# A hybrid attention and RWKV-7 step on one core: one small store ahead of a load, one activation ahead of a copy, and the stores at a stage's end on SyncE

## The chip, the cores and the metric

The kernel runs on one core of a Trainium2 chip. The core has five engines with an instruction queue each: TensorE (PE, with its weight loads shown as PEld), VectorE (DVE), ScalarE (ACT), GpSimd (POOL) and SyncE (SP), which here issues most DMAs. The engines wait for each other through semaphores. The metric is the device time of one execution in microseconds; the median of the runs of a kernel counts.

## The reference, cut to what matters

One layer of a streaming encoder is computed for a prompt of 2048 rows and for 8 running streams of 16 rows each (together 17 tiles of 128 rows, tile 16 being the streams):

```python
proj = rms_norm(h, norm_gain) @ w_in
att, rcols, g_r = split_projection(proj)
q, k, v, g_a = attn_qkv(att, q_norm_gain, k_norm_gain)
o_a = chunk_band_attention(q, k, v, rel_pos_bias)       # streams: attention over a cache
prev = jnp.concatenate([jnp.zeros_like(rcols[:, :1]), rcols[:, :-1]], axis=1)
o_r, S = rwkv_branch(rcols, prev, S0, g_r, ...)          # a recurrence over time with state S
z = jnp.concatenate([o_a * silu(g_a), o_r], axis=-1)     # o_r holds silu(g_r) already
h = h + z @ w_out
```

The outputs are both updated sequences, the new keys and values, the recurrent states and the last projected rows.

## The kernel before, in words

`program` runs four stages, one after the other. Each is a block of instruction streams, one for each engine. At a block's end all engines meet, GpSimd clears the block's semaphores (`clear_semaphores`), and only then does the next block's first instruction run on any engine. Waits for stores whose semaphores are in `Shared` are left to the end of the last block.

1. `attention_phase` (about 0 to 545 us): for each tile the q, k, v projection (each fp32 product as three products of fp32r halves, "hi" and "lo"), the norms and the chunked attention. Beside it the normalised, transposed x is made for the later stages: ScalarE finds each row's 1/rms (`norm_stats`), SyncE stores those 128 numbers in memory (`store_rstd`, L233) and reads them back spread over all partitions (`load_row`, L238), GpSimd multiplies (`norm_x`, L337 and L340), and SyncE stores the tile (`store_xT`, L246). `load_x` (L225) brings the next tile's rows for ScalarE; it waits for the sum of squares of the tile before, and `store_rstd` for that tile's finished 1/rms, two small ScalarE instructions later.
2. `rwkv_projection_phase` (to about 855 us): the token-shifted projection.
3. `rwkv_phase` (to about 1567 us): the recurrence, with the gate projection beside it. Its instruction order is written as generators: each `yield` gives a place on a scale of some 40 units for a tile, and `merged` takes the pieces of all generators of an engine in the order of these numbers. In the last step (t = DEC = 16) `out` begins the output product for tiles 0 and 1: `split_w` halves w_out into `out_w_hi` (ScalarE) and `out_w_lo` (GpSimd for k = 0 and 1, VectorE after), `open_gates` applies silu to a tile's gates (`z_gate`), `store_y` writes y.
4. `output_phase` (about 1568 us to the end): the output product for the other 15 tiles, and the cached attention of the 8 streams.

At the end of stage 3 these meet: `store_y(0, j)` on SyncE; the new states of the streams (`out_wkv_sample_new`, L1501, two stores); the rows of `o_rwkv` of tile 16 (`tail`, L1490, four stores), which stage 4 reads back only for its last tile; and the two halves of y of tile 1, stored by ScalarE (L1776) after VectorE's last additions (`add_x(1, j)`, L1951), the second of which ends VectorE's stream.

Of the kernel before, what the change touches and what calls it, by code (L numbers as in the profile page):

```python
# [22 lines left out]
P = 128  # L23
D = 1024
# [34 lines left out]
def rows_of(dram, width):  # L59

    return dram.rearrange("b s d -> (b s) d")
# [70 lines left out]
def attention_phase(nc, io, shared):  # L132
    with ExitStack() as ctx:
# [88 lines left out]
        def _(sp):  # L222
            def load_x(n):
                wait(sp, x_sumsq, n)
                sp.dma_start(x_tok[:], x_rows(n)).then_inc(x_loaded, 16)  # L225

            def load_xT(n):
                wait(sp, xT_stored, 16 * (n - 2))
                sp.dma_start(xT[n % 3][:], io["x_T"][n]).then_inc(xT_loaded[n % 3], 16)

            def store_rstd(n):
                sp.wait_ge(x_rstd, n + 1)
                sp.dma_start(io["rstd"][n].rearrange("(p o) -> p o", o=1), rstd[:, n:n + 1]).then_inc(rstd_stored, 16)  # L233

            def load_row(n):
                sp.wait_ge(rstd_stored, 16 * (n + 1))
                wait(sp, x_by_row, n)
                sp.dma_start(row[:], io["rstd"][n].rearrange("(o p) -> o p", o=1).broadcast_to([P, P])).then_inc(row_loaded, 16)  # L238
# [5 lines left out]
            def store_xT(n):  # L244
                sp.wait_ge(x_normed, n + 1)
                sp.dma_start(io["xT"][n], xT[n % 3][:]).then_inc(xT_stored, 16)  # L246

            def store_kv(t):
                rows = slice((t - 12) * P, (t - 11) * P)
                sp.wait_ge(k_kept, t - 11)  # L250
                sp.dma_start(io["k_prompt_new"][0, 0, :, rows, :].rearrange("h s d -> s h d"),
                             k_out[:].rearrange("p (h d) -> p h d", h=H)).then_inc(k_stored, 16)
                sp.wait_ge(proj_read, 3 * (t + 1))
                sp.dma_start(io["v_prompt_new"][0, 0, :, rows, :].rearrange("h s d -> s h d"),
                             v[:, t % RING, :].rearrange("p (h d) -> p h d", h=H)).then_inc(v_stored, 16)

            def store_o(t):
                sp.wait_ge(out_ready, t + 1)
                sp.dma_start(io["o_att"][t * P:(t + 1) * P, :], o_tok[:].rearrange("p h d -> p (h d)")).then_inc(out_stored, 16)
# [34 lines left out]
            for t in range(TILES):  # L294
                more = t + 2 <= DEC
                if t >= 12:
                    store_kv(t)
                if t + 3 <= DEC:
                    load_x(t + 3)
                if more:  # L300
                    store_rstd(t + 2)
                    load_row(t + 2)
                if t > 1:
                    store_o(t - 2)
                if more:
                    store_xT(t + 2)
                if t + 5 <= DEC:
                    load_xT(t + 5)
# [785 lines left out]
def rwkv_phase(nc, io, shared):  # L1094

    with ExitStack() as ctx:
# [5 lines left out]
        def sem(name):  # L1102
            held.append(ctx.enter_context(nc.semaphore("r_" + name)))
            return held[-1]

        def sb2(name, shape):
            return [sb(f"{name}{i}", shape) for i in range(2)]

        def sems2(name):
            return [sem(f"{name}{i}") for i in range(2)]  # L1110
# [49 lines left out]
        gate_out = sb2("gate_out", [P, AW])  # L1160
# [83 lines left out]
        go_loaded, x_half_loaded, y_stored = sems2("go_loaded"), sems2("x_half_loaded"), shared.y_stored  # L1244
        z_opened, z_gated, z_turned, z_hi_ready, z_lo_ready = sem("z_opened"), sem("z_gated"), sem("z_turned"), sem("z_hi_ready"), sem("z_lo_ready")
        y_summed, y_added = sem("y_summed"), sem("y_added")
# [63 lines left out]
        OUT_X = tuple(slice(j * 512, (j + 1) * 512) for j in range(2))  # L1310
# [19 lines left out]
        LAST_TAIL = 34  # L1330
# [46 lines left out]
        def _(sp):  # L1377
# [32 lines left out]
            def load_out_w(k):  # L1410
                sp.dma_start(out_raw[k % 4][:].rearrange("p k n -> p (k n)"), io["w_out"][0, k * P:(k + 1) * P, :]).then_inc(shared.out_w_loaded[k % 4], 16)
# [7 lines left out]
            def load_x_half(n, j):  # L1419
                sp.dma_start(gate_out[j][:], rows_of(io["x_prompt"], D)[n * P:(n + 1) * P, OUT_X[j]]).then_inc(x_half_loaded[j], 16)  # L1420

            def store_y(n, j):
                sp.wait_ge(y_added, 2 * n + j + 1)
                sp.dma_start(rows_of(io["y_prompt"], D)[n * P:(n + 1) * P, OUT_X[j]], gate_out[j][:]).then_inc(y_stored[j], 16)
# [29 lines left out]
            def out(t, u, mode):  # L1454
                yield 0
                for k in range(4, KT):
                    sp.wait_ge(shared.out_w_lo, k - 3)
                    load_out_w(k)
                for j in range(2):
                    sp.wait_ge(gate_stored[j], 16 * (DEC + 1))  # L1460
                    load_x_half(0, j)
                yield 19
                for n in range(2):
                    sp.wait_ge(z_turned, 2 * n + 2)
                    load_go(2 + n, shared.g_loaded[n], shared.o_loaded[n])
                for j in range(2):
                    yield 31 + j
                    store_y(0, j)
                    sp.wait_ge(y_stored[j], 16)
                    load_x_half(1, j)  # L1470

            def mix(t, u, mode):

# [8 lines left out]
                load_xs(t, u, slice(0, 4), r_loaded)  # L1482

            def tail(t, u, mode):
                yield 17.5 if mode == "p" else 45.5 - LAST_TAIL
                need(sp, t, "out")
                for n in range(NCH):
                    rows = io["o_rwkv"][t * P + n * CH:t * P + (n + 1) * CH, :].rearrange("l (c g d) -> g l c d", g=2, d=HD)
                    for g in range(2):
                        sp.dma_start(rows[g], y_tok[half(g), cols_of(n)].rearrange("p (c d) -> p c d", c=PAIRS)).then_inc(o_stored, 16)  # L1490
# [124 lines left out]
        def _(act):  # L1615
# [116 lines left out]
            def open_gates(n, loaded, opened):  # L1732
                act.wait_ge(loaded, 48 if loaded is go_loaded[n % 2] else 16)
                nc.scalar.activation(z_gate[n % 2][:], z_gate[n % 2][:], ACT.Silu).then_inc(opened, 1)

            def out(t, u, mode):
                def split_w(k):
                    if k == 0:
                        act.wait_ge(gate_written, 2 * (DEC + 1))
                    act.wait_ge(shared.out_w_loaded[k % 4], 16 * (k // 4 + 1))  # L1740
                    nc.scalar.activation(out_hi[:, k, :], out_raw[k % 4][:].rearrange("p k n -> p (k n)"), ACT.Copy).then_inc(shared.out_w_hi, 1)

                def round_z(n, i):
                    act.wait_ge(z_turned, 2 * n + i + 1)
                    nc.scalar.activation(z_hi[n][:, 4 * i:4 * i + 4, :].rearrange("p k n -> p (k n)"), ps_job[i][:], ACT.Copy).then_inc(z_hi_ready, 1)

                yield 0.2
                split_w(0)
                open_gates(0, go_loaded[0], z_opened)
                split_w(1)  # L1750
                yield 3.3
                open_gates(1, go_loaded[1], z_opened)
                for i in range(2):
                    round_z(0, i)
                yield 7.35
                for k in range(2, 4):
                    split_w(k)
                yield 8.5
                for k in range(4, KT):
                    split_w(k)  # L1760
                yield 10.6
                for i in range(2):
                    round_z(1, i)
                yield 22
                for n in range(2):
                    open_gates(2 + n, shared.g_loaded[n], shared.silu_ready)
                act.preload_act_table_set(ACT_TABLES)
                for i in range(2):
                    yield 31.6 + 2 * i
                    act.wait_ge(y_summed, 2)  # L1770
                    act.wait_ge(z_turned, 5 + i)
                    nc.scalar.activation(x_hi[:, 4 * i:4 * i + 4, :].rearrange("p k n -> p (k n)"), ps_job[1][:], ACT.Copy).then_inc(shared.z_first_hi, 1)
                for j in range(2):
                    yield 50 + j
                    act.wait_ge(y_added, 2 + j + 1)
                    act.dma_start(rows_of(io["y_prompt"], D)[P:2 * P, OUT_X[j]], gate_out[j][:]).then_inc(y_stored[j], 16)  # L1776

            tiles(act, front, back, mix, tail, gates, first_gates, out)

# [931 lines left out]
```

## Time and profile before

| | |
|---|---|
| median of 3 runs | 1772.42 us (1771.13 to 1773.47) |
| the profiled execution | 1771.13 us, its span 1769.3 us |
| PE busy | 1707.2 us (96%), mean granted clock 0.985 |
| DVE, ACT, POOL busy | 828.6, 799.4, 417.3 us |
| bytes moved by DMA | 170.88 MB, mean 97 GB/s |

The span runs from the first to the last instruction of the profiled execution; the time of the execution is 1.8 us more. A row's "[idle before <- releaser]" says how long its engine sat idle and what ended that. SPq and ACTq are DMA issues on the queues of SyncE and ScalarE: their duration is the time of the issue, not of the transfer. A merged row ("x4") stands for several instructions in a row, from the start of the first.

### The profile page before, as it was taken

Reading aid. Unit: us, or ns where it says so; the run is one execution under the profiler, and the core shown is the slowest. Engines: PE = TensorE matmul, PEld = TensorE weight load, DVE = VectorE, ACT = ScalarE, POOL = GpSimd, SP = SyncE. Lnnn points to the kernel's source line nnn. Section 1 sums busy time; section 2 is a strip of 40 time slices with the busy share of each in tenths; the row PEclk is TensorE's granted clock in tenths of the full one; section 3 lists DMA queues with packets and bytes.
Section 4 is the critical chain, followed back from the end, with each engine's and each line's share of the span. In section 5 each row is a group of like instructions: output and inputs, shape, how many; then the busy total and the mean of one; then the engine's idle time right before and its main releaser. Section 6 shows DMA issues by size and latency. Waiting matters only on the chain. (4 is left out here: it accounts for less than half of the span.)

```text
span 1769.3 us, 48548 instructions
## 1 busy us (share of the span) xinstructions
PE 1707.2 (96%) x21338; PEld 1398.7 (79%) x21338; DVE 828.6 (47%) x1198; ACT 799.4 (45%) x1656; POOL 417.3 (24%) x282
## 2 busy tenths in 40 slices
PE   6999999999998999999889999999999999889999
PEld 5778888888887888999667777787777777667787
DVE  4345444444444311223446565555565556643432
ACT  5556666665655322223434444444444444423420
POOL 3332221122110000000213544334454334320000
PEclk9999999999999999999889999999999999899999
DMA  6322211112134412214311212212212213466652
GB/s 228 110 73 81 59 52 68 56 57 74 44 109 174 154 61 87 85 61 146 112 48 52 72 52 66 67 52 63 60 52 75 58 53 108 143 252 230 205 176 87
DMA packets 119138, 170.88 MB, mean 97 GB/s; under 512 B 39568, under 2 KB 78992, under 8 KB 118672
## 3 DMA queue, kind: packets, MB, share of 16 engines
q1 hardware_dynamic: 109280, 152.76, 26.8%
q10 hardware_dynamic: 9648, 15.01, 2.3%
q8 instruction: 169, 2.77, 0.7%
q14 instruction: 41, 0.34, 0.1%
HBM read 113.21 MB, written 55.06 MB: 95 GB/s over the span
## 5 line engine op out<-in xcount | busy, mean ns | idle before, releaser
L652 PE MATMUL a_ps_proj<-a_w_hi,a_x_hi 128*128 128x512 f32 x384 | 155.8, 406 | 0.0
L652 PE MATMUL a_ps_proj<-a_w_hi,a_x_lo 128*128 128x512 f32 x384 | 150.2, 391 | 0.0
L652 PE MATMUL a_ps_proj<-a_w_lo,a_x_hi 128*128 128x512 f32 x384 | 149.6, 390 | 0.0
L1056 DVE SCALAR_TENSOR_TENSOR j_out<-j_ps,j_rest,j_part 128x512 f32<-128x512 f32 (+2 forms) x65 | 41.9, 645 | 220.4 <-ACT j_last_cols L1004 170.0
L562 DVE SCALAR_TENSOR_TENSOR a_stage<-a_ps_s,a_new_bias 128x256 f32<-128x256 f32 x64 | 27.2, 424 | 229.0 <-PE a_ps_s L679 229.0
L2222 PE MATMUL r_ps_gate<-gate_w_hi,gate_x_hi 128*128 128x512 f32 x272 | 116.5, 428 | 4.6 <-PEq L66 3.4
L2222 PE MATMUL r_ps_gate<-gate_w_lo,gate_x_hi 128*128 128x512 f32 x272 | 116.4, 428 | 0.0
L2222 PE MATMUL r_ps_gate<-gate_w_hi,gate_x_lo 128*128 128x512 f32 x272 | 116.3, 428 | 0.0
L1002 ACT ACTIVATE j_part<-j_last_cols,j_shift_in 128x1 f32<-128x1 f32 x65 | 19.2, 296 | 212.8 <-PE j_ps L1081 212.8
L1862 DVE TENSOR_TENSOR r_w_mat<-r_ps_w,consts 128x512 f32<-128x512 f32 x83 | 57.3, 691 | 106.0 <-PE r_ps_w L2106 106.0
L337 POOL TENSOR_TENSOR a_xT<-a_xT,a_row 128x1024 f32<-128x1024 f32 x17 | 40.4, 2374 | 251.6 <-DMA a_row<-scratch_rstd 241.0
L445 ACT ACTIVATE a_stage<-a_stage,a_small 128x640 f32<-128x640 f32 (+4 forms) x128 | 95.9, 753 | 0.9 <-DVE a_small L570 0.9
L679 PEld LDWEIGHTS a_ps_s<-a_kT,a_qT 64*128 64x128 f32 x592 | 59.8, 186 | 33.1 <-issue 28.0
L570 DVE TENSOR_REDUCE a_small<-a_stage 128x2 f32<-128x1280 f32 (+4 forms) x64 | 84.5, 1320 | 2.2
L652 PEld LDWEIGHTS a_ps_proj<-a_w_hi,a_x_lo 128*128 128x128 f32 x384 | 72.1, 188 | 16.1
L652 PEld LDWEIGHTS a_ps_proj<-a_w_lo,a_x_hi 128*128 128x128 f32 x384 | 72.4, 189 | 13.3
L679 PE MATMUL a_ps_s<-a_kT,a_qT 64*128 64x128 f32 (+3 forms) x592 | 81.7, 389 | 1.0 <-ACT a_kT L436 0.8
L652 PEld LDWEIGHTS a_ps_proj<-a_w_hi,a_x_hi 128*128 128x128 f32 x384 | 72.2, 188 | 13.2 <-issue 0.2
L454 ACT ACTIVATE a_stage<-a_ps_p 128x1024 f32<-128x1024 f32 (+3 forms) x60 | 56.5, 942 | 52.9 <-PE a_ps_s L701 52.9
L713 PE MATMUL a_ps_out<-a_stage,a_v 128*64 128x128 f32 x1120 | 75.3, 278 | 1.4 <-ACT a_stage L456 1.4
L1511 POOL MEMSET r_g_run<- 128x544 f32 x1 | 0.6, 557 | 308.2 <-POOLq L66 308.2
L713 PEld LDWEIGHTS a_ps_out<-a_stage,a_v 128*64 128x64 f32 x1120 | 59.8, 136 | 9.5 <-ACT a_stage L456 1.6
(383 smaller groups left out, 4690.2 us busy)
## 6 DMA issues: line engine op xcount, KB each, us to landing
a_xT<-in_x_T SPq DMA_DIRECT2D x17, 512.0 KB, 3.6
scratch_xT<-a_xT SPq DMA_DIRECT2D x17, 512.0 KB, 2.6
raw<-scratch_xT SPq DMA_DIRECT2D x17, 512.0 KB, 4.6
scratch_gates<-r_gate_out SPq DMA_DIRECT2D x34, 256.0 KB, 2.4
z_gate<-scratch_gates SPq DMA_DIRECT2D x17, 512.0 KB, 4.3
xs<-scratch_xs_T SPq DMA_DIRECT2D x15, 576.0 KB, 4.3
a_x<-in_x_prompt SPq DMA_DIRECT2D x16, 512.0 KB, 4.5
scratch_xs_T<-j_out ACTq DMA_DIRECT2D x39, 192.0 KB, 1.9
```

The costliest lines, as they stand in the source:

```text
L337: nc.gpsimd.tensor_tensor(xT[n % 3][:], xT[n % 3][:], by_token, ALU.mult).then_inc(x_by_row, 1)
L445: nc.scalar.activation(probs[s % 2][:, e, lo * P:WIN], probs[s % 2][:, e, lo * P:WIN], ACT.Exp, bias=neg_max[s % 2][:, e:e + 1], accum_out ...
L454: nc.scalar.activation(pT[:, :, lo:SLOTS - 1, :].rearrange("p e j n -> p e (j n)"), ps_p[:].rearrange("p (e n) -> p e n", e=2)[:, :, lo * ...
L562: nc.vector.scalar_tensor_tensor(out=out[:, :, OLD:WIN], in0=ps_new, scalar=SCALE, in1=new_bias[:, 2 * c:2 * c + 2, :], op0=ALU.mult, op1= ...
L570: nc.vector.tensor_reduce(neg_max[s % 2], out[:, :, lo * P:WIN], AX_X, ALU.max, negate=True).then_inc(max_ready, 1)
L652: mm = nc.tensor.matmul(ps_proj[:], a[n % 2][:, k, :], w[:, k, g * AW:(g + 1) * AW], start=(k == 0 and i == 0), stop=(k == KT - 1 and i == 2))
L679: return nc.tensor.matmul(out, qT[t % 2][half, c, :], kT[half, c, r:r + b - a, :].rearrange("p j n -> p (j n)"), start=True, stop=True)
L713: mm = nc.tensor.matmul(ps_out[e * HD:(e + 1) * HD, c * P:(c + 1) * P], v[:, ring(t, j), h * HD:(h + 1) * HD], pT[:, e, j, :], start=(j == ...
L1002: nc.scalar.activation(part[j][:, 0:1], last_cols[:, c, (g + 1) % 2:(g + 1) % 2 + 1], ACT.Copy, scale=share)
L1056: last = nc.vector.scalar_tensor_tensor(out=out[j][:, 0:n], in0=ps[j][:, 0:n], scalar=rest[:, c:c + 1], in1=part[j][:, 0:n], op0=ALU.mult, ...
L1862: nc.vector.tensor_tensor(w_mat, heads(ps_w[:]), level, ALU.mult).then_inc(w_ready, 1)
L2222: mm = nc.tensor.matmul(ps_gate[:], x[:, k, :], w[:, j, k, :], start=i == 0, stop=i == 3 * KT - 1)
```

## The change

Four edits. In the attention stage SyncE issues `store_rstd` ahead of `load_x`. At the end of stage 3 the stores of tile 1 of y go from ScalarE's queue to SyncE's, at key 50. The key of the streams' `tail` on SyncE goes from 45.5 to 17.5 + 34 = 51.5 (`later` adds `LAST_TAIL`), behind all other pieces. At the start of `out` ScalarE has `open_gates(0)` ahead of `split_w(0)`.

```diff
@@ attention_phase, SyncE, for each tile t
                 if t >= 12:
                     store_kv(t)
+                if more:
+                    store_rstd(t + 2)
                 if t + 3 <= DEC:
                     load_x(t + 3)
                 if more:
-                    store_rstd(t + 2)
                     load_row(t + 2)
@@ rwkv_phase, SyncE, out
                     store_y(0, j)
                     sp.wait_ge(y_stored[j], 16)
                     load_x_half(1, j)
+                yield 50
+                for j in range(2):
+                    store_y(1, j)
@@ rwkv_phase, SyncE
             def tail(t, u, mode):
-                yield 17.5 if mode == "p" else 45.5 - LAST_TAIL
+                yield 17.5
                 need(sp, t, "out")
@@ rwkv_phase, ScalarE, out
                 yield 0.2
+                open_gates(0, go_loaded[0], z_opened)
                 split_w(0)
-                open_gates(0, go_loaded[0], z_opened)
                 split_w(1)
@@ rwkv_phase, ScalarE, out, at its end
-                for j in range(2):
-                    yield 50 + j
-                    act.wait_ge(y_added, 2 + j + 1)
-                    act.dma_start(rows_of(io["y_prompt"], D)[P:2 * P, OUT_X[j]], gate_out[j][:]).then_inc(y_stored[j], 16)
```

What this moves on each engine is shown at three places. The first is SyncE's stream in the attention stage, t = 0, before the change:

```order
L225 DMA a_x<-in_x_prompt 128x1024
L233 DMA scratch_rstd<-a_rstd 128x1
L238 DMA a_row<-scratch_rstd 128x128
L246 DMA scratch_xT<-a_xT_77 128x1024
L229 DMA a_xT_77<-in_x_T 128x1024
```

and after it:

```order
L233 DMA scratch_rstd<-a_rstd 128x1
L225 DMA a_x<-in_x_prompt 128x1024
L238 DMA a_row<-scratch_rstd 128x128
L246 DMA scratch_xT<-a_xT_77 128x1024
L229 DMA a_xT_77<-in_x_T 128x1024
```

The first two have changed places; the same holds for each tile up to t = 13 (for t = 14 there is no row tile left to load).

The second place is SyncE's end of stage 3 and its first issue of stage 4, before the change (the branches are the block's end and the next one's start):

```order
L1501 DMA out_wkv_sample_new<-r_states 512x1x256
L1490 DMA scratch_o_rwkv<-r_y_tok 256x1x64 x4
L1501 DMA out_wkv_sample_new<-r_states 512x1x256
L1096 UNCONDITIONAL_BRANCH
L2357 UNCONDITIONAL_BRANCH
L2362 DMA z_gate_66<-scratch_gates 128x1024
```

and after it, where `store_y` is at L1425 and the tail at L1494:

```order
L1505 DMA out_wkv_sample_new<-r_states 512x1x256 x2
L1425 DMA out_y_prompt<-r_gate_out 128x512 x2
L1494 DMA scratch_o_rwkv<-r_y_tok 256x1x64 x4
L1097 UNCONDITIONAL_BRANCH
L2357 UNCONDITIONAL_BRANCH
L2362 DMA z_gate_66<-scratch_gates 128x1024
```

Two stores of y have come onto this queue, and the four stores of `o_rwkv` have moved from the middle to its end.

The third place is ScalarE at the start of `out` in step 16, before the change (`raw_49` and `raw_50` are rows of w_out, `z_gate_66` and `z_gate_67` the gates of tiles 0 and 1, `r_y_mat` a copy that the recurrence's first level needs):

```order
L1741 ACTIVATE out_w_hi<-raw_49 128x1024
L1734 ACT_TABLE_LOAD
L1734 ACTIVATE z_gate_66<-z_gate_66 128x1024
L1741 ACTIVATE out_w_hi<-raw_50 128x1024
L1677 ACTIVATE r_y_mat<-r_ps_q 128x512
L1734 ACTIVATE z_gate_67<-z_gate_67 128x1024
```

and after it:

```order
L1738 ACT_TABLE_LOAD
L1738 ACTIVATE z_gate_66<-z_gate_66 128x1024
L1745 ACTIVATE out_w_hi<-raw_49 128x1024
L1745 ACTIVATE out_w_hi<-raw_50 128x1024
L1681 ACTIVATE r_y_mat<-r_ps_q 128x512
L1738 ACTIVATE z_gate_67<-z_gate_67 128x1024
```

The table load and the first silu stand ahead of the first copy of w_out; all that follows is as it was. The streams of TensorE, VectorE and GpSimd are unchanged.

## Rows read from the trace of the kernel before

**Rows 1.** Windows: stretch, its length, busy time of each engine, granted clock, DMA share, GB/s.

```profile
100.00:500.00 400.00, 398.56 (x2933) 325.87 (x2932) 194.09 (x223) 245.06 (x503) 94.84 (x45) 1.00 0.21 65
1569.00:1769.00 200.00, 196.39 (x1176) 156.59 (x1174) 69.26 (x115) 59.17 (x68) 1.48 (x3) 0.99 0.57 200
```

**Rows 2.** Timeline of SP, attention stage: start, duration, engine, line, operation.

```profile
215.31 0.33 SPq L233 DMA_DIRECT2D scratch_rstd<-a_rstd  x1
223.59 0.33 SPq L238 DMA_DIRECT2D a_row<-scratch_rstd  x1
...
478.25 0.34 SPq L233 DMA_DIRECT2D scratch_rstd<-a_rstd  x1
486.62 0.34 SPq L238 DMA_DIRECT2D a_row<-scratch_rstd  x1
```

**Rows 3.** Timeline around the end of stage 3: ACT, SP, DVE and PE.

```profile
1562.05 5.09 ACTq L1776 DMA_DIRECT2D out_y_prompt<-r_gate_out  x2
1563.73 2.50 SPq L1490 DMA_DIRECT2D scratch_o_rwkv<-r_y_tok  x4
1564.93 1.23 DVE L1906 TENSOR_TENSOR r_states<-r_states,r_g_last 128x1024 f32<-128x1024 f32 x1
1566.08 0.68 DVE L1951 TENSOR_TENSOR r_gate_out<-r_gate_out,r_ps_job 128x512 f32<-128x512 f32 x1
1566.27 0.61 SPq L1501 DMA_DIRECT2D out_wkv_sample_new<-r_states  x1
1568.49 0.33 SPq L2362 DMA_DIRECT2D z_gate<-scratch_gates  x1
1568.68 0.47 PE L2555 MATMUL o_ps_y<-out_w_hi,gate_x_hi 128*128 128x512 f32 x1 [2.98 <-PEq L66]
```

**Rows 4.** The issues of three lines: duration ns min/median/max, first and last start.

```profile
L1490 SPq DMA_DIRECT2D scratch_o_rwkv<-r_y_tok x68: 513/616/1417, 954.3 to 1565.6; - x68
L1501 SPq DMA_DIRECT2D out_wkv_sample_new<-r_states x2: 576/594/613, 1557.5 to 1566.3; - x2
L1776 ACTq DMA_DIRECT2D out_y_prompt<-r_gate_out x2: 344/362/379, 1562.0 to 1566.8; - x2
```

**Rows 5.** Windows of low clock after the starts of stages 2, 3 and 4.

```profile
546.10:552.10 6.00, 5.99 (x14) 4.76 (x15) 4.25 (x6) 5.32 (x7) 0.27 (x2) 0.50 0.45 118
856.30:862.60 6.30, 6.28 (x25) 4.76 (x26) 0.94 (x1) 2.49 (x9) 1.92 (x6) 0.50 0.29 89
1569.30:1572.60 3.30, 3.30 (x10) 2.51 (x9) 0.00 (x0) 0.00 (x0) 1.18 (x2) 0.51 0.99 315
```

**Rows 6.** Timeline of ACT, PE and DVE at the start of `out`.

```profile
1498.89 1.28 ACT L1734 ACT_TABLE_LOAD   x1
1500.69 1.06 ACT L1734 ACTIVATE z_gate<-z_gate 128x1024 f32<-128x1024 f32 x1 [0.52 <-DMA z_att<-scratch_o_rwkv]
1501.65 1.04 ACT L1741 ACTIVATE out_w_hi<-raw 128x1024 fp32r<-128x1024 f32 x1
1502.60 0.58 ACT L1677 ACTIVATE r_y_mat<-r_ps_q 128x512 f32<-128x512 f32 x1
...
1504.09 1.68 PE L2106 MATMUL r_ps_w<-r_y_mat,r_bm 64*64 64x64 f32 x32
...
1506.52 0.65 DVE L1862 TENSOR_TENSOR r_w_mat<-r_ps_w,consts 128x512 f32<-128x512 f32 x1
...
1514.78 2.00 ACT L1741 ACTIVATE out_w_hi<-raw 128x1024 fp32r<-128x1024 f32 x2
```

**Rows 7.** Timeline of POOL and DVE: instructions of both at the same time.

```profile
1502.77 2.46 POOL L1609 TENSOR_TENSOR out_w_lo<-raw,out_w_hi 128x1024 fp32r<-128x1024 f32 x1 [1.47 <-ACT out_w_hi L1741]
1503.64 1.61 DVE L1914 TENSOR_SCALAR r_small<-r_small 128x8 f32<-128x8 f32 x1
...
1552.73 1.78 DVE L1906 TENSOR_TENSOR r_states<-r_states,r_g_last 128x1024 f32<-128x1024 f32 x1
1553.38 2.02 POOL L1562 TENSOR_TENSOR r_w_mat<-r_v_tok,r_bonus 128x512 f32<-128x512 f32 x1
```

## The prediction, made before the changed kernel ran

> **What bounds the kernel now.** I read the page first, then the busy time by stretch, the waits of TensorE, and the timelines of SyncE, ScalarE and VectorE wherever the change puts a hand. In the attention stage TensorE is busy for 398.6 of 400 us at full clock, and in the output stage for 196.4 of 200 us [rows 1]. There only what TensorE itself waits for can move the end, and an engine beside it may be early or late by some us without effect. In stage 3 TensorE is a link of a chain, and between two stages it stands still: before stage 4 it was idle for 2.98 us, because a block's first instruction waits until every engine has ended the block before [rows 3]. So the question for each edit is whether it reaches TensorE, or the engine that ends stage 3 last.
>
> Stage 3 ends like this [rows 3, 4]. VectorE ends its last addition at 1566.08 + 0.68 = 1566.76. ScalarE waits for it and issues the second half of y of tile 1, until 1562.05 + 5.09 = 1567.14 (the merged row is two issues of 0.34 to 0.38 us and the wait between them). SyncE ended at 1566.27 + 0.61 = 1566.88. The last of the three is ScalarE, at 1567.14. SyncE's first issue of stage 4 starts at 1568.49, so the handover takes 1.35 us, and TensorE's first product starts 0.19 us behind it.
>
> **The change, part by part.**
>
> *The stores at the end of stage 3.* I walk SyncE's new queue with the durations of before. The second store of the streams' states is released by VectorE at 1564.93 + 1.23 = 1566.16, and is issued from about 1566.20 for 0.59 us, to 1566.79. The first half of y is long ready (its store started at 1562.05 before), and is issued until about 1567.23 (0.38 us plus a gap of 0.05). The second half is released at 1566.76, already past, and goes until about 1567.70. Behind them now stand the four stores of `o_rwkv`, ready since 1563.73 or earlier, which took 2.50 us as a row of four, 0.62 us each [rows 3, 4]. With the gap SyncE ends at about 1570.25. Nothing else of the block ends later than 1566.76. The end of the stage moves from 1567.14 to 1570.25: **+3.1 us**. Nothing hides it: TensorE has no work of stage 3 left and can't begin stage 4. Before, the same four issues lay between 1563.73 and 1566.23, beside the last products, and cost nothing.
>
> The bounds: with the shortest of the 68 issues of this line (0.51 us) the four take 2.05 us and the sum is +2.7. If one of them meets a full queue, as the longest did (1.42 us), it is +3.9. I take the row of this very place, 2.50 us.
>
> The Trainium skill says (DMA: Bandwidth & Descriptors, "Issuing engines are not separate DMA queues") that spreading DMAs over issuing engines saves only the sequencer's issue time, usually small beside the transfer. The rows agree on what it saves. Read as "small, so free", the rule would put this part at 0, and the sum at the clock's term or less.
>
> *TensorE's clock.* After each of the three handovers TensorE ran for a while at half clock, 1.2 instead of 2.4 GHz: for 6.0 us, 6.3 us and, at stage 4, 3.3 us, here only from 0.6 us behind its first product on [rows 3, 5]. The idle times ahead were 2.3 to 3.4 us. Now it is idle for 2.98 + 3.1 = 6.1 us, longer than any of these. A stretch at half clock loses half its length, and the low stretch of stage 4 cost 1.65 us. If the next is as long as the mean of the three, 5.2 us, it costs 2.6: **+1.0 us**. The bounds are 0 (3.3 us again) and +1.5 (6.3 us). I take the mean, since the shortest one belongs to a start that was still fast at first.
>
> *What stage 4 makes of a later start.* It is bound by TensorE, and its loads all start behind the same handover, so they move with it. The DMA engines are full at its start (share 0.99 in the third row of [rows 5]), and the 0.25 MB of `o_rwkv` and 0.5 MB of y are issued closer to it. But they are issued while nothing else is, in 3 us that did not exist before. I cost this at 0, with up to 1 us above if a load that TensorE waits for lands late; no such wait is in stage 4 now. The stored rows of `o_rwkv` are read only for the last tile.
>
> *The 1/rms store ahead of the load, 14 times.* With the 512 KB load ahead of it the store took from 215.31 to 223.59, 8.3 us, until the read behind it was issued; in the tile without such a load it took from 478.25 to 486.62, 8.4 us [rows 2]. So the load ahead is not what makes it slow. The read of the row, and GpSimd's two products, come at best some tenths earlier, and they feed only the stored x of later stages. The load goes out less than 1 us later, and is wanted a whole tile later. TensorE's 400 us have 1.4 us of idle time in all to give back. I cost it at 0, from -0.4 us to +0.2 us.
>
> *The silu ahead of the first copy.* The silu of tile 0 did not start at 1500.17, when the table was loaded, but at 1500.69, when the last transfer of its tile had landed [rows 6]. With the copy (1.05 us) moved behind it, it starts at the same 1500.69: no gain. What is behind is pushed: the two copies run to about 1503.65, and the copy of `r_y_mat`, which was at 1502.60, comes at about 1503.55 and ends at 1504.15. TensorE's products with it started at 1504.09 and would start at about 1504.2. They ended at 1505.77, and VectorE took their result only at 1506.52, being busy with other work. So 0.1 us is late there with 0.7 us of slack. GpSimd gets its first half of w_out at 1502.7, behind the silu, and subtracts twice in a row, to about 1507.6 (2.46 us each, [rows 7]). SyncE reloads the two buffers behind that, so some us later than before; ScalarE wants them at 1514.78 and after, over 7 us on [rows 6]. I cost the edit at 0, from -0.1 to +0.3.
>
> **The sum.** 3.1 + 1.0 + 0 + 0 + 0 = +4.1 us. The profiled execution took 1771.13 us (1.8 more than its span), so its like would take 1775.2. It was the fastest of three; on the median of 1772.42 it is **1776.5 us**. Two tenths of a per cent, 3.5 us, is about what a measurement of this kernel can tell from no change. The sum lies just above.
>
> **The rivals.**
>
> *The four issues are not waited for.* If the handover doesn't wait for the issue of stores already handed to the queue, or they go out faster behind each other, SyncE ends at about 1567.7: +0.6 us, with the clock's 0 to 1.0 behind it, say +1.0 in all, 1773.4 us. Against it speaks that in [rows 3] each issue starts where the one ahead ends. For it, that no handover in this trace was held by SyncE with so many issues. This is "no change".
>
> *Faster.* The one place from which the change could win is ScalarE at 1500.69. If the last transfer of tile 0 landed 0.5 us earlier, for instance, the silu would start as soon as the table is loaded, which is now 1.05 us earlier, and the chain of VectorE and TensorE behind it with it: at most -1.0 us. Together with the four issues not being waited for and no longer low clock this gives 1772.0 or less. It decides only when the landing moves ahead of 1500.17, and nothing in the change makes it.
>
> *VectorE is held by GpSimd.* The little product of L1914 took 1.61 us and ended at 1505.25, as GpSimd's subtraction did at 1505.23 [rows 7]: the one waited for the other. Now GpSimd has a second subtraction directly behind. If VectorE had to wait for both, its chain would be 2.4 us later, and TensorE's next products with it: +6.5 us in all, 1778.9. Against it: at 1553.4 GpSimd also had two instructions in a row, and VectorE's L1906, held since 1552.73, got in between: it ended at 1554.51 and GpSimd's second, of half the size of the subtraction, took 2.02 us, so that it will have waited in its turn. The Trainium skill states the same (SBUF — State Buffer, "Who interferes with whom"): the pair of ports that both share goes to whoever comes first, for the whole instruction. By that rule the trace's pattern repeats and VectorE, which waits already, is next.
>
> *The queue fills.* Eight issues in a row and then twelve loads of stage 4: if several are held as the longest was (1.42 us), or the loads land later, the sum is +5.5 to +7, 1778.5.
>
> **How the numbers follow.** The forecast (SyncE's tail sets the handover, +2.7 to +5.4) gets 0.62; the issues not waited for 0.16; faster 0.04; VectorE held 0.09; the queue filled 0.09. Within the forecast a good two thirds lie above 3.5 us, the rest below. Slower by over 0.2%: 0.43 + 0.09 + 0.09 = 0.61. Within: 0.19 + 0.16 = 0.35. Faster: 0.04. The range reaches down to 1773.2, which takes in the upper half of "not waited for", and up to 1779.5, for the two rivals above; some 2 in 10 are left out at the two ends.
>
> **What would show it.** In the new profile SyncE's row of four stores of `o_rwkv` stands last in stage 3 and ends at 1570 to 1571; the first issue of stage 4 follows 1.2 to 1.5 us later; TensorE's idle time ahead of its first product there is 5.7 to 6.8 us instead of 2.98, and the low clock behind it lasts 3.3 to 6.3 us. TensorE in the attention stage is as busy as before. The silu of tile 0 starts within 0.2 us of the same place, VectorE's L1914 still ends with GpSimd's first subtraction, and the last product of stage 3 ends where it did. I am wrong if stage 4 starts less than 2 us later, if the last product of stage 3 moves by more than 0.5 us, or if a wait of TensorE for a load appears in stage 4.

## The result, and the profile after

The changed kernel takes 1785.72 us (median of 6 runs, 1780.75 to 1791.63), the one before 1771.78 us (6 runs, 1767.76 to 1775.64). The ratio is 1.0068, 95% interval 1.0047 to 1.0090: slower, by 12 us (8 to 16). It compares the runs themselves and isn't the quotient of the two medians, which would be 1.0079; the same holds for the ratios further down, and the gains and losses of whole kernels in us are worked out from them. The forecast was 1776.5 us in a range of 1773.2 to 1779.5: the sign was right and the size was not.

The profiled execution of the changed kernel took 1780.9 us (span 1779.1), close to its fastest, and 9.8 us more than that of before. By stages, from the starts of the blocks on TensorE:

| stretch | before | after | difference |
|---|---|---|---|
| attention stage | 546.11 | 554.03 | +7.9 |
| projection stage | 310.21 | 307.36 | -2.9 |
| stage 3 to VectorE's last addition | 710.44 | 709.63 | -0.8 |
| from there to TensorE's first product of stage 4 | 1.92 | 6.16 | +4.2 |
| stage 4 | 200.62 | 201.92 | +1.3 |

The fourth row is the edit that the forecast priced. The first is not: it is a new wait in the stage that was called untouched. Its chain in three views of the changed kernel. First SyncE's issues in the rounds of tiles 0 and 1 (start, us, queue, line, output and input):

```profile
61.55 0.43 SPq L233 DMA_DIRECT2D scratch_rstd<-a_rstd  x1
62.02 0.43 SPq L225 DMA_DIRECT2D a_x<-in_x_prompt  x1
70.68 0.32 SPq L238 DMA_DIRECT2D a_row<-scratch_rstd  x1
...
85.61 0.32 SPq L233 DMA_DIRECT2D scratch_rstd<-a_rstd  x1
85.97 0.87 SPq L225 DMA_DIRECT2D a_x<-in_x_prompt  x1
94.58 0.32 SPq L238 DMA_DIRECT2D a_row<-scratch_rstd  x1
```

Then ScalarE's statistics of one tile (the first row, at the end of the round of tile 1) and of the next (the row at 99.00):

```profile
83.86 1.07 ACT L382 ACTIVATE a_x<-a_x 128x1024 f32<-128x1024 f32 x1
...
88.78 0.38 ACT L457 ACTIVATE a_stage<-a_ps_s 128x256 f32<-128x256 f32 x1
99.00 1.06 ACT L382 ACTIVATE a_x<-a_x 128x1024 f32<-128x1024 f32 x1 [9.83 <-DMA a_x<-in_x_prompt]
```

And TensorE's longest waits there (what waited, for what, us in total, times, longest; the second stands in the trace of before too), with its first products behind the first wait:

```profile
PE a_ps_p L699 <- ACT a_stage L446: 6.5, 1, 6.5
PE a_ps_out L714 <- ACT a_stage L457: 1.4, 1, 1.4
...
101.96 1.11 PE L699 MATMUL a_ps_p<-a_ident,a_stage 128*128 128x128 f32 x4 [6.45 <-ACT a_stage L446]
```

ScalarE needs this tile 4 us after it has freed the buffer, not a round later. For tiles 2 and 3 the statistics stand at the end of a round, from tile 4 on at the start of one (the two places of `norm_stats` in ScalarE's loop). So the last of the first kind and the first of the second stand back to back, at 83.86 and, with the data there, at about 89.2. The load between them was issued at 85.97 and landed at 99.0, 13 us later. TensorE then stood for 6.45 us.

The wait costs more than its own length. The granted clock fell to half (1.2 instead of 2.4 GHz) at 98.6 us, while TensorE stood, and stayed there until 105.4, so that its first 3.5 us of work ran at half speed: the four products of the last row took 1.11 us, where e4 (below), at full clock, took 0.66 for the same four. That is another 1.7 us. The rest of the +7.9 has no part in the change: TensorE was already 1.4 us late at 47 us, before the first moved pair, after a stretch at half clock near 41 to 44 us, and the trace of before has a wait of 1.44 us for VectorE, at 124.58, that this one lacks. 6.45 + 1.7 + 1.4 - 1.44 is about 8.1, close to the 7.9 measured.

Over the whole stage, from 60 to 560 us, the time from issue to landing of x (`a_x`) is, before and then after:

```profile
DMA to landing us min/median/max: 3.4/4.0/9.4
```

```profile
DMA to landing us min/median/max: 8.4/12.3/13.3
```

The busy share of the DMA engines rises as well. The first row here answers to the first of [rows 1]. The other three are stretches of 100 us inside it. The same bytes are moved (58 to 63 GB/s), and the engines are busy for 0.38 to 0.42 of the time (last but one column):

```profile
100.00:500.00 400.00, 398.04 (x2894) 325.65 (x2896) 190.37 (x220) 246.62 (x513) 89.53 (x43) 0.99 0.39 63
...
160.00:260.00 100.00, 100.00 (x726) 80.99 (x726) 48.51 (x54) 62.07 (x125) 19.94 (x9) 1.00 0.42 58
260.00:360.00 100.00, 100.00 (x771) 82.72 (x770) 48.83 (x56) 60.98 (x124) 19.94 (x9) 1.00 0.42 59
360.00:460.00 100.00, 100.00 (x729) 81.48 (x727) 49.47 (x56) 61.57 (x125) 22.12 (x11) 1.00 0.38 63
```

Before, the share in these three was:

```profile
160.00:260.00 100.00, 100.00 (x724) 81.05 (x725) 49.43 (x54) 60.86 (x124) 20.29 (x9) 1.00 0.21 59
260.00:360.00 100.00, 100.00 (x760) 82.50 (x762) 47.27 (x54) 62.14 (x125) 20.59 (x10) 1.00 0.19 61
360.00:460.00 100.00, 100.00 (x744) 81.63 (x741) 48.12 (x56) 60.88 (x123) 23.01 (x12) 1.00 0.23 64
```

TensorE is at 100 of 100 us in each of these rows of both kernels: outside the one place, the late load costs nothing. The row of 400 us hardly shows the loss at all (398.04 us busy, 398.56 before), since 4.5 of the 6.45 us lie ahead of its start.

The end of stage 3 of the changed kernel answers to [rows 3]: VectorE's last addition, SyncE's row, and TensorE's first product of stage 4.

```profile
1570.34 0.68 DVE L1951 TENSOR_TENSOR r_gate_out<-r_gate_out,r_ps_job 128x512 f32<-128x512 f32 x1
...
1570.44 0.55 SPq L1505 DMA_DIRECT2D out_wkv_sample_new<-r_states  x1
1571.04 1.61 SPq L1425 DMA_DIRECT2D out_y_prompt<-r_gate_out  x2
1572.70 2.74 SPq L1494 DMA_DIRECT2D scratch_o_rwkv<-r_y_tok  x4
1576.99 0.33 SPq L2362 DMA_DIRECT2D z_gate<-scratch_gates  x1
...
1577.18 0.77 PE L2555 MATMUL o_ps_y<-out_w_hi,gate_x_hi 128*128 128x512 f32 x1 [7.17 <-PEq L66]
```

SyncE's four stores end last, at 1575.44, and the next block's first issue follows 1.55 us later. The first product ran at 0.77 us instead of 0.47, so already at the low clock.

### The profile page after: what moved, and what is told of

It reads as the page before. It is cut to its first block and busy times, and to the rows that moved or that the text cites. A ratio compares the mean times of both kernels' runs of the same rounds, so it can differ in the third digit from the quotient of the medians.

```text
span 1779.1 us, 48548 instructions
## 1 busy us (share of the span) xinstructions
PE 1704.3 (96%) x21338; PEld 1397.0 (79%) x21338; DVE 827.6 (47%) x1198; ACT 798.0 (45%) x1656; POOL 417.3 (23%) x282
## 6 DMA issues: line engine op xcount, KB each, us to landing
a_x<-in_x_prompt SPq DMA_DIRECT2D x16, 512.0 KB, 12.3
```

## The experiments

Theory 1: most of the loss is the load of x behind the small store, at the one place where it is wanted at once, and the rest is SyncE's tail. Theory 2: all of it is the tail and the clock behind it. Each kernel was timed in 5 to 12 runs against 19 to 35 of the kernel before, whose medians were 1771.87 us beside e1 to e4, 1774.41 beside e5 to e8, 1771.09 beside e9 to e12, and 1772.21 beside e13 and e14. "Landing" is the median from issue to landing of x from 60 to 560 us, "stage 2" the first product of the projection stage, "idle" TensorE's wait ahead of stage 4.

| kernel | median us | ratio (95% interval) | landing | stage 2 | idle |
|---|---|---|---|---|---|
| e1, store ahead of load | 1778.36 | 1.0041 (1.0021-1.0061) | 10.9 | 550.5 | 2.98 |
| e2, both edits at the end of stage 3 | 1775.21 | 1.0016 (0.9999-1.0033) | 3.5 | 545.4 | 7.17 |
| e3, silu first | 1771.09 | 0.9990 (0.9972-1.0009) | 3.4 | 544.5 | 2.96 |
| e4, as e1, store on ScalarE's queue | 1775.62 | 1.0016 (0.9996-1.0036) | 8.0 | 548.4 | 2.99 |
| e5, y on SyncE | 1774.69 | 1.0015 (0.9993-1.0037) | 3.6 | 544.7 | 4.48 |
| e6, tail last | 1777.82 | 1.0023 (1.0005-1.0042) | 3.5 | 546.0 | 6.23 |
| e7, as e1, statistics late | 1832.62 | 1.0325 (1.0300-1.0350) | 12.3 | 607.1 | 2.93 |
| e8, statistics late | 1811.94 | 1.0209 (1.0180-1.0239) | 3.5 | 589.7 | 2.96 |
| e9, as e1, tile 1 alone | 1778.15 | 1.0043 (1.0025-1.0062) | 3.5 | 556.5 | 2.95 |
| e10, as e1, all but tile 1 | 1770.08 | 0.9993 (0.9974-1.0012) | 11.8 | 545.8 | 2.95 |
| e11, 64 values ahead | 1778.48 | 1.0045 (1.0029-1.0060) | 10.1 | 555.6 | 2.96 |
| e12, the change without e1's part | 1776.28 | 1.0032 (1.0014-1.0051) | 3.6 | 546.2 | 7.18 |
| e13, 1 value ahead | 1771.52 | 1.0009 (0.9992-1.0025) | 3.4 | 548.6 | 2.96 |
| e14, 16 values ahead | 1775.32 | 1.0004 (0.9986-1.0022) | 4.9 | 547.2 | 2.97 |

**The edits one by one: e1, e2, e3 and e12.** e1 is the first hunk of the diff alone, e2 the second, third and fifth, e3 the fourth, e12 all but the first.

> Only the store of 1/rms stands ahead of the load of x; the other three edits are left out. Theory 1 (the load of x behind the store of four bytes per row lands some 8 us later; this is wanted too early once, between tiles 1 and 2): the load of L225 lands about 12 us after its issue in the median, ScalarE waits 8 to 10 us for a_x at 89 to 99 us, TensorE waits 5 to 7 us for ScalarE near 102 us, stage 2 starts at 552 to 554 instead of 546.1, and the kernel takes 5 to 9 us more than before. Theory 2 (all of the loss is at the end of stage 3 and the clock behind it): within 1 us of before.

> Only the two edits at the end of stage 3: y of tile 1 stored by SyncE, and the stores of the stream's output behind it. Theory 1 (this is the smaller part of the loss): stage 2 starts at 546.1 as before, the last store of L1494 ends at 1570 to 1571, stage 4 starts 3 to 4 us later than before, +3 to +5 us in all. Theory 2 (all of the loss is here): +9 to +12 us.

> Only the silu of tile 0 ahead of the first copy. My step in the prediction: within 0.5 us of before. Rival (VectorE held by GpSimd's two subtractions, or w_out reloaded too late): the last product of stage 3 ends 1 to 3 us later than 1565.7 and the kernel takes 1 to 3 us more.

> The changed kernel with the load of x ahead of the store again, that is the silu and both edits at the end of stage 3. If the parts add up: what e2_stage_end and e3_silu_first give together, +1 to +4 us over before, with stage 2 starting at 544.5 to 546.5 and TensorE idle for 7.2 us before stage 4. If the parts need each other for the loss of 12 us: +8 us or more.

The store ahead of the load costs 7.3 us (3.7 to 10.8) by itself; the three other edits together cost 5.7 us (2.5 to 9.0). The sum, 13.0, is the 12 us of the whole change within its interval: the store and the rest add up. e12 lies above its range of +1 to +4 all the same, and above what e2 (+2.8, -0.2 to +5.8) and e3 (-1.8, -5.0 to +1.6) give singly; the intervals are too wide to say whether those two need each other. Theory 2 falls: e2 has only the smaller part of the loss, with its last store ending at 1571.08. In e1 the time is as expected, and the four signs in the profile lie a little below their ranges (10.9, 7.9, 4.6 us, and 550.5). ScalarE waits for x and TensorE for ScalarE:

```profile
ACT a_x L382 <- DMA a_x<-in_x_prompt: 7.9, 1, 7.9
PE a_ps_p L699 <- ACT a_stage L446: 4.6, 1, 4.6
```

The silu is within its interval of no change, as its step said.

**One round, and all but one: e9 and e10.** The diff is that of e9; e10 has the opposite condition.

```diff
+                if more and t == 1:          # e10: t != 1
+                    store_rstd(t + 2)
                 if t + 3 <= DEC:
                     load_x(t + 3)
                 if more:
-                    store_rstd(t + 2)
+                    if not (t == 1):         # e10: t != 1
+                        store_rstd(t + 2)
                     load_row(t + 2)
```

> The store of 1/rms stands ahead of the load of x in one round of 14 only, that of tile 1. If the attention stage loses at this one place: the load of that round lands 10 to 13 us after its issue and all others after 3 to 5, ScalarE waits 5 to 10 us for a_x near 89 to 99 us, TensorE waits 3 to 7 us near 102 us, stage 2 starts at 549 to 554, and the time is that of e1_rstd_first, 5 to 8 us above before. If the loss is spread over the rounds (the DMA engines being held): less than 1.5 us above before.

> The store ahead of the load in all rounds but that of tile 1. One place: the loads land after 10 to 13 us in the median, yet ScalarE waits for a_x no longer than 2 us, TensorE doesn't wait for it, stage 2 starts at 544.5 to 546.5, time within 1.5 us of before. Spread: 4 us or more above before.

This settles the place. With 13 of the 14 rounds swapped x lands after 11.8 us in the median, and the time is that of before (0.9993). With one round swapped it lands after 3.5 us in the median, and the kernel loses 7.6 us (4.4 to 11), all that e1 loses. Stage 2 starts later in e9 than I expected (556.5): behind the wait of 6.1 us TensorE ran at half clock for 5.6 us of work, and it was 3.3 us late at 49 us already, before the moved pair. ScalarE's statistics of the tile in question, in e9 and then in e10, where they follow at once:

```profile
100.54 1.06 ACT L384 ACTIVATE a_x<-a_x 128x1024 f32<-128x1024 f32 x1 [9.52 <-DMA a_x<-in_x_prompt]
```

```profile
89.12 1.06 ACT L384 ACTIVATE a_x<-a_x 128x1024 f32<-128x1024 f32 x1
```

**What the store does to the load: e4, e11, e13 and e14.** In e4 ScalarE issues the store, on its own queue, behind the activation that makes the values; in the round of tile 1 store and load are issued at the same 86.62 us. In the others SyncE stores part of the 128 values ahead of the load and the rest behind it, and the read of the row waits for both parts. The diff is that of e11, cut to the order of the issues:

```diff
+                if more:
+                    store_rstd(t + 2, 0, P // 2)     # e13: 0, 1    e14: 0, 16
                 if t + 3 <= DEC:
                     load_x(t + 3)
                 if more:
-                    store_rstd(t + 2)
+                    store_rstd(t + 2, P // 2, P)     # the rest
```

> As e1_rstd_first, but ScalarE issues the store of 1/rms, on its own queue, right behind the activation that makes it; SyncE's order of the rest is that of e1. If the load is late because it stands behind the store in one queue: the load of L225 lands after 4 to 5 us again, TensorE doesn't wait at 102 us, stage 2 starts within 1.5 us of 546.1, and the time is within 2 us of before. If it is late because the writes of four bytes hold the 16 DMA engines themselves: it lands after 8 to 12 us where the two meet, and the loss of e1 stays.

> As e1_rstd_first, but only the first 64 of the 128 values of 1/rms are stored ahead of the load and the other 64 behind it. If each write of four bytes has its price (about 8 us for 128): the load of x lands after 7 to 9 us in the median, between the 4.5 us of before and the 10.8 to 12.3 us with 128 ahead, the wait of TensorE near 102 us is 1 to 3 us, and the time is 2 to 4 us above before. If the store has a fixed price whatever its size (one round trip to memory that all behind it waits for): the load lands after 10 to 12 us as in e1, and the time is that of e1 or more.

> As e11_half_ahead, but a single value of 1/rms is stored ahead of the load of x and the other 127 behind it. If the late load is a price of each small write, or of each that stands ahead of it on the same DMA engine: the load lands after 4 to 6 us in the median and the time is within 2 us of before. If any store ahead holds the load until it has been written out, whatever its size: the load lands after 8 to 12 us, and the time is 5 to 8 us above before, as with 128.

> Sixteen values ahead of the load, 112 behind it. Price per write: the load lands after 4.5 to 6 us, 1 us (an eighth of the 8 us for 128) later than without a store ahead. Fixed price: 8 to 12 us.

With 0, 1, 16, 64 and 128 values ahead x lands after 3.5, 3.4, 4.9, 10.1 and 10.9 us (0 from e2; 12.3 us for 128 in the changed kernel, with the same code there). A store of one value ahead costs nothing, so it isn't a fixed price for having a store in front. The price grows with the number of values, by 0.09 us for each at 16 and 0.10 at 64. From 64 to 128 it hardly grows; my expectation for 64 (7 to 9 us) was too low, and why it flattens isn't shown. Nor is it shown what of a value's write has the price, or how the writes are spread over the DMA engines.

The time of e11, +8.0 us (5.1 to 10.6) where I expected 2 to 4, isn't the landing alone. The two half stores end later than one whole store: in the round of tile 0 the row is read at 76.53 us instead of 71.48, and what hangs on it follows later, so that SyncE comes to the load of x in the round of tile 1 only here, 4.2 us after the 1/rms that it waits for:

```profile
90.93 0.58 SPq L225 DMA_DIRECT2D a_x<-in_x_prompt  x1
```

It landed 8.6 us after that; ScalarE waited 9.2 us, and TensorE 5.8 (1 to 3 expected). In e13 ScalarE doesn't wait for x, and the late start of stage 2 (548.6) has another source: TensorE waits 2.54 us for VectorE at 126.77, as it does for 1.44 us at that place before. In e14 ScalarE waits 1.6 us.

These four stage-wide views stand for the landings, of e13, e14, e11 and e4 in this order:

```profile
DMA to landing us min/median/max: 3.2/3.4/4.9
```

```profile
DMA to landing us min/median/max: 4.6/4.9/8.7
```

```profile
DMA to landing us min/median/max: 8.5/10.1/11.7
```

```profile
DMA to landing us min/median/max: 5.2/8.0/9.2
```

The last row is the store on another queue: 8.0 us, two fifths of the way back from 10.9 to 3.5. So part of the delay is the place in the queue, and part stays when only the DMA engines are shared. The raised share goes with the first part: in e4 the DMA engines are busy for 0.16 to 0.21 of the three stretches shown above, no more than before, while the share rises with the number of values ahead (0.21 to 0.24 with one, 0.27 to 0.32 with 16, 0.41 to 0.44 with 64). Both of my alternatives for e4 were too simple; TensorE's wait fell to 1.5 us, and the clock stayed at full behind it. The time, 1.0016 (0.9996 to 1.0036), takes in no change and the lower part of e1's interval, so by itself it decides nothing. The Trainium skill (DMA: Bandwidth & Descriptors, "Issuing engines are not separate DMA queues") says that DMAs run on the same 16 DMA engines and interleave there, whoever starts them: the second part agrees with that. The same page of the Trainium skill ("Specifications") puts the smallest transfer for line rate at 512 B or more. The four-byte values are far below; the price per value is what the runs show.

**The parts of the end of stage 3: e5 and e6.** e5 is the moved stores of y alone (second and fifth hunk), e6 the tail's key alone (third hunk).

> Only y of tile 1 stored by SyncE; the four stores of L1490 stay beside the last products. By the walk of SyncE's queue: it ends at about 1567.7 instead of 1566.9, the handover to stage 4 moves by +0.6 us, and the time is within 1 us of before. Rival (the second store of y is what holds SyncE for longer): SyncE ends later than 1569 and the handover moves by over 2 us.

> Only the four stores of the stream's output moved to the end; ScalarE still stores y of tile 1. By the walk of the queue: SyncE ends at about 1566.8 + 2.5 = 1569.3, stage 4 starts 2 to 3 us later against the end of the last addition of stage 3 than before, and the time is +2 to +3.5 us. If it is +4 us or more, the y stores have no part in the loss at all.

SyncE's last rows of stage 3 and its first of stage 4, in e5 and then in e6:

```profile
1565.77 0.62 SPq L1504 DMA_DIRECT2D out_wkv_sample_new<-r_states  x1
1566.43 1.62 SPq L1424 DMA_DIRECT2D out_y_prompt<-r_gate_out  x2
1569.49 0.33 SPq L2361 DMA_DIRECT2D z_gate<-scratch_gates  x1
```

```profile
1573.56 0.55 SPq L1501 DMA_DIRECT2D out_wkv_sample_new<-r_states  x1
1574.16 3.43 SPq L1490 DMA_DIRECT2D scratch_o_rwkv<-r_y_tok  x4
1579.15 0.34 SPq L2362 DMA_DIRECT2D z_gate<-scratch_gates  x1
```

TensorE's idle time ahead of stage 4 grows by 1.5 us in e5 (I expected 0.6), by 3.25 us in e6 (2 to 3), and by 4.2 us with both (3.1). Two stores of y take 1.62 us on SyncE, not 0.8: 0.63 and 0.95 us, right behind the store of the states. I had taken the 0.38 us of ScalarE's queue [rows 4], where each stood alone. It isn't the engine that makes the difference, since SyncE's own store of the other tile's y, with nothing close ahead of it, is as short; in the changed kernel:

```profile
1559.41 0.33 SPq L1425 DMA_DIRECT2D out_y_prompt<-r_gate_out  x1
```

Behind a row of other issues it took 0.44 us (e5, at 1528.51) to 1.12 (before, at 1528.75). What sets the time there isn't shown. The time of e6 by itself, +4 us (0.9 to 7.4), would also fit a loss in which the stores of y have no part; the idle time in e5 says that they have one.

**Another place for the statistics: e7 and e8.** e8 puts the statistics of tile t+2 at the end of every round, e7 does so on top of e1. The diff shows what the edit amounts to:

```diff
-                    if more and t > 1:
-                        norm_stats(t + 2)
...
-                if t < 2:
+                if more:
                     norm_stats(t + 2)
```

> The store of 1/rms ahead of the load, as in e1_rstd_first, but the statistics of tile t+2 come at the end of every tile's round, not only of tiles 0 and 1, so that no load of x is wanted sooner than a round after its issue. If the loss in e1 is the one place between tiles 1 and 2: the load still lands 10 to 13 us after its issue, but ScalarE waits for it no longer than 2 us, TensorE doesn't wait for ScalarE near 102 us, and stage 2 starts within 1.5 us of 546.1; time within 1.5 us of e8_stats_late. If the store in front costs in every tile (the DMA engines being held, the row of 1/rms later): stage 2 still starts 3 us or more later.

> The kernel before with the statistics of tile t+2 at the end of every round, to stand beside e7_rstd_first_stats_late. Expected within 1.5 us of before, stage 2 starting within 1 us of 546.1: the wait of 1.8 us of ScalarE for a_x at 89 us goes, and something of ScalarE moves in its place. If the place of the statistics matters by itself, it shows here.

Both expectations of the time failed, by 37 us for e8. The control is not neutral. SyncE's store of 1/rms, and behind it the row's read and the store of the attention's output, come half a round later; VectorE then waits for that store in nearly every round, and TensorE for VectorE. From e8:

```profile
DVE a_o L582 <- DMA scratch_o_att<-a_o: 113.7, 12, 10.6
ACT a_stage L454 <- PE a_ps_s L701: 61.2, 51, 4.3
PE a_ps_s L701 <- DVE a_stage L562: 27.4, 12, 3.6
```

In the kernel before VectorE waits for it once. What e7 does show is that the waits of ScalarE for x and of TensorE for ScalarE are gone though x lands after 12.3 us; its time can't be used, and why it is 20.7 us above e8 wasn't settled.

## Why the prediction was right or wrong, point by point

**The failed step** is the 1/rms store ahead of the load: "The load goes out less than 1 us later, and is wanted a whole tile later", costed at 0, from -0.4 to +0.2 us. Its first half looked at the issue and not at the landing. The issue is 0.5 us later; the landing is 7 to 8 us later. I had the store's own time with and without a load ahead in [rows 2], and asked only whether the load slows the store. The other direction was never priced, though 8.4 us for 512 bytes was the oddest number of the table. Its second half is false in one round of 14: `norm_stats` has two places in ScalarE's loop, `t < 2` and `t > 1`, and where the one hands over to the other the buffer is wanted 4 us after it is free. The trace of before showed that place: ScalarE waited there for x, its only such wait from 60 to 550 us. I had read the waits of TensorE, where 1.8 us of ScalarE don't appear. And a wait of that length takes the clock with it: 1.7 us in the changed kernel, where the forecast looked at the clock only behind the handovers. Measured: +7.3 us (3.7 to 10.8), where 0 stood. The sign that I had named for this stage, TensorE as busy as before, could hardly have shown it, read over 100 to 500 us.

**"TensorE's 400 us have 1.4 us of idle time in all to give back"** was a bound for a gain. I let it stand for the loss too; a loss has no such bound.

**The stores at the end of stage 3**: the mechanism was right, the term too small, and this part is what the forecast's right sign rests on. SyncE's four stores end last (e2, e12 and the changed kernel alike), and the handover moves by 4.2 us, not 3.1. The two stores of y cost 0.8 us more than I took, for their place in the row of issues, the four of `o_rwkv` 0.24 us more (2.74 instead of 2.50), and the handover behind SyncE takes 1.55 us, not 1.35. The rival "not waited for" is refuted by each of e2, e5, e6 and e12.

**The clock**, +1.0 us in a range of 0 to 1.5: stage 4 takes 201.92 us instead of 200.62 in the changed kernel, +1.3. But e2 and e12, with the same idle time of 7.2 us and the same slow first product, take 200.6 and 200.4 us. The price was right: stage 4 is longer by half of the time at half clock. From its first product on this time is 3.4 us before (200.62 us for the stage), 6.2 in the changed kernel (201.92), 5.7 in e5 (201.62), 5.0 in e6 (201.36), 3.5 in e2, 3.0 in e12, and 0 in e14 (199.0). The length was the guess, and the idle time ahead doesn't set it: e5 has 4.5 us of idle time and e2 and e12 have 7.2. That the changed kernel's profile came close to +1.0 is luck.

**The silu** costs nothing (e3, 0.9990, 0.9972 to 1.0009), and the rival "VectorE is held" did not come. In the changed kernel GpSimd has its two subtractions in a row, the first until 1511.96, and VectorE gets in behind the first, as at 1553.4 in the kernel before:

```profile
1509.49 4.78 POOL L1613 TENSOR_TENSOR out_w_lo<-raw,out_w_hi 128x1024 fp32r<-128x1024 f32 x2 [6.42 <-ACT out_w_hi L1745]
```

```profile
1510.36 1.62 DVE L1914 TENSOR_SCALAR r_small<-r_small 128x8 f32<-128x8 f32 x1
```

L1914 ends at 1511.98 and the pair at 1514.27, as the rule of the Trainium skill cited in the prediction has it (SBUF — State Buffer, "Who interferes with whom").

**The queue fills**: partly. No issue was held as long as 1.42 us, but in e6 the four took 3.43 us.

## What to carry to other kernels

Price a reordered pair of DMAs by landing and in both directions: what the second does to the first, and what the first does to the second. Here the store whose time was out of proportion to its bytes (8 us for 512) held the load behind it for 7 to 8 us. Take an issue's duration from a place with like issues close ahead, not from one where it stands alone. When a wait of TensorE is priced, look also at the granted clock behind it. And look up, for every round of the loop, who wants a moved transfer and when, above all where a loop's body changes its form: one round of 14 carried all of the loss, and the only wait of ScalarE for this buffer in the trace of before stood just there.

## What the runs showed of the hardware

A store of 128 values of four bytes, one from each partition, makes a 512 KB load behind it in the same queue land after 10.9 to 12.3 us instead of 3.5, and after 8.0 with the store on another queue. One value ahead makes no difference, 16 make 1.4 us.

TensorE's clock fell to half during its waits for the late load: behind waits of 4.6 (e1), 6.1 (e9), 5.8 (e11) and 6.45 us (the changed kernel) its first 3.0, 5.6, 5.8 and 3.5 us of work ran at half clock; behind 1.5 us (e4) it stayed at full clock.

The projection stage follows the same price as stage 4. With no half clock at its start (the changed kernel, e1, e14) it takes 307.3 to 307.4 us; with 3.1 to 3.8 us of it (e2, e5, e6, e9 to e13) 308.8 to 309.1; with 5.6 to 6.2 us (before, e3, e4) 310.0 to 310.2. That is the -2.9 us of the table above: scatter of the clock and not the change, since e4, e9 and e11 have the moved store too and the half clock with it. What decides how long the clock is low at a start isn't shown. The scatter is larger than such terms: stage 3 and its handover, the same code as before in e1, e4, e9, e10, e11, e13 and e14, took from 707.9 us (e10) to 720.7 us (e14), against 712.4 before. One profile's total can't place 2 us of a whole kernel, and a dozen runs leave 3 to 4 us open on either side; the small terms here rest on single waits and stages in the traces.
